# Third expert weight loaded from ScalarE's DMA queue instead of SyncE's

## What is computed

```python
def _expert_choice(h, router_w, w1, w3, w2):
    ...
    gate, idx = lax.top_k(aff.T, C)
    xe = xs[idx]
    he = jax.nn.silu(jnp.einsum('ecd,edf->ecf', xe, w1)) * jnp.einsum('ecd,edf->ecf', xe, w3)
    ye = jnp.einsum('ecf,efd->ecd', he, w2) * gate[..., None].astype(h.dtype)
    out = jnp.zeros_like(xs).at[idx.reshape(-1)].add(ye.reshape(-1, D))
    return out.reshape(B, L, D)
...
    x = x + gate2 * _expert_choice(h, lp['router_w'], lp['exp_w1'], lp['exp_w3'], lp['exp_w2'])
```

## Time and profile before

| | |
|---|---|
| median of 3 runs | 1870.99 us (1865.37 to 1871.74) |
| the profiled execution's own time | 1873.86 us |
| its span, first to last instruction | 1872.0 us |
| mean granted TensorE clock over the span | 0.967 |
| TensorE matmul busy | 1765.5 us (94%) |
| VectorE, ScalarE, GpSimd busy | 672.1, 350.8, 155.3 us |
| moved by DMA | 542.20 MB, of which 501.16 MB on SyncE's queue |

### The profile page before, as it was taken

The page is one execution under the profiler, slowest core; times in us unless marked ns, Lnnn a source line. Parts: engine busy times, 40 slices in busy tenths (PEclk is TensorE's granted clock), DMA queues, the critical chain, the costliest instruction groups (busy, mean ns, idle before and its releaser), DMA issues.

```text
span 1872.0 us, 50720 instructions
## 1 busy us (share of the span) xinstructions
PE 1765.5 (94%) x23010; PEld 1179.4 (63%) x23010; DVE 672.1 (36%) x1562; ACT 350.8 (19%) x781; POOL 155.3 (8%) x141
## 2 busy tenths in 40 slices
PE   5999988979999999999889998898999999999996
PEld 3776767846666666666557776686566666556653
DVE  5543767542121111112166367765121111112114
ACT  3410365310000000000142115722000000000001
POOL 0200030100000000000002002210000000000000
PEclk8999999979999999999979999998999999999996
DMA  9668201289999999999943722035999999999994
GB/s 357 216 219 314 92 2 46 102 320 415 395 401 399 405 397 405 398 401 399 362 131 137 269 71 91 5 121 200 399 398 397 400 396 406 395 402 398 395 372 158
DMA packets 91919, 542.20 MB, mean 290 GB/s; under 512 B 7536, under 2 KB 12658, under 8 KB 68676
## 3 DMA queue, kind: packets, MB, share of 16 engines
q1 hardware_dynamic: 80444, 501.16, 67.6%
q0 software_dynamic: 10464, 36.51, 6.8%
q10 hardware_dynamic: 808, 1.39, 0.2%
HBM read 515.50 MB, written 23.53 MB: 288 GB/s over the span
## 4 chain that ended last, share of the span: by engine, by line
PE 75%; DMA 14%; DVE 6%; ACT 2%; issue 2%; POOL 1%; ACTq 0%; DVEq 0%; SPq 0%; POOLq 0%
PE bank L1198 43%; DMA ring<-in_exp_w 12%; PE bank L848 11%; PE bank L1035 5%; PE bank L723 3%; PE bank L750 2%; PE bank L1056 1%; PE bank L994 1%; PE bank L1217 1%; PE bank L1073 1%; PE bank L979 1%; DMA arena_z<-xn_dram,icur 1%; PE bank L883 1%; PE bank L1106 1%; PE bank L789 1%
## 5 line engine op out<-in xcount | busy, mean ns | idle before, releaser
L1198 PE MATMUL bank<-ring,arena_u 128*32 128x256 f32 x12288 | 680.0, 381 | 1.9 <-DVE arena_u L2140 1.3
L1198 PEld LDWEIGHTS bank<-ring,arena_u 128*32 128x32 f32 x12288 | 399.5, 110 | 264.3 <-issue 6.0
L1198 PE MATMUL bank<-ring,arena_z 128*32 128x256 f32 x6144 | 340.6, 381 | 14.8 <-DMA ring<-in_exp_w 9.5
L1198 PEld LDWEIGHTS bank<-ring,arena_z 128*32 128x32 f32 x6144 | 205.5, 110 | 145.8 <-issue 11.1
L2172 DVE SCALAR_TENSOR_TENSOR arena_z<-bank,gateT,gate 80x512 f32<-80x512 f32 (+1 forms) x60 | 34.2, 609 | 560.1 <-PE bank L1198 560.1
L1512 ACT ACTIVATE arena_z<-bank 128x512 f32<-128x512 f32 x30 | 17.9, 597 | 623.5 <-PE bank L1198 623.5
L2149 DVE TENSOR_TENSOR arena_z<-arena_z,bank 128x512 f32<-128x512 f32 x64 | 48.5, 838 | 199.1 <-PE bank L1198 199.1
L1035 PE MATMUL bank<-ring_r 128*128 128x512 f32 x320 | 100.8, 396 | 0.3 <-DVE arena_h_r L1899 0.3
L677 POOL DMA_INDIRECT x_res<-arena_z,iscat x30 | 43.2, 1439 | 670.6 <-DVE arena_z L2175 670.6
L1523 ACT ACTIVATE arena_z<-bank 32x256 f32<-32x256 f32 (+1 forms) x90 | 34.0, 377 | 295.6 <-PE bank L1198 294.9
L848 PE MATMUL bank<-ring_r,arena_h_r 128*128 128x512 f32 (+1 forms) x240 | 87.2, 363 | 0.0
(11 more groups left out here) (303 smaller groups left out, 1906.4 us busy)
## 6 DMA issues: line engine op xcount, KB each, us to landing
ring<-in_exp_w SPq DMA_DIRECT2D x180, 2048.0 KB, 21.6
ring<-in_ada_w SPq DMA_DIRECT2D x23, 2048.0 KB, 9.5
ring<-in_exp_w SPq DMA_DIRECT2D x48, 512.0 KB, 14.3
ring<-in_w_in SPq DMA_DIRECT2D x7, 2048.0 KB, 19.4
ring<-in_w_out SPq DMA_DIRECT2D x2, 4096.0 KB, 13.0
x_res<-arena_z POOLq DMA_DIRECT2D x10, 512.0 KB, 3.3
xn_dram<-arena_u POOLq DMA_DIRECT2D x10, 512.0 KB, 2.9
arena_z<-x_res POOLq DMA_DIRECT2D x5, 512.0 KB, 3.8
```

What stands on the lines that cost most here:

```text
L1198: mm = pe.matmul(group_out(out, g, slice(q * 32, q * 32 + 32)), x(c, t), slot[s][:, c, w * QUARTER:(w + 1) * QUARTER], start=(c == 0 and g ...
```

## The change

ScalarE issues the loads of the third weight for experts 1 to 15; SyncE's loop loses them. The two waits and the two transfers for each load stay what they were. The load is placed in ScalarE's program ahead of `gated` of the same expert.

```diff
@@ SyncE
                 fill(0, "exp_w1", 1, 0)
-                fill(1, "exp_w3", 1, w3_at(0))
                 with sp.Fori(1, EXPERTS - 1) as e:
                     fill(0, "exp_w1", e + 1, w1_next_at(e) - 3)
                     fill(2, "exp_w2", e, w2_at(e) - 3)
-                    fill(1, "exp_w3", e + 1, w3_at(e))
                 fill(2, "exp_w2", EXPERTS - 1, w2_at(EXPERTS - 2))
@@ ScalarE
+                def w3_next(e):
+
+                    for h in range(2):
+                        act.wait_ge(chunk_used, AHEAD + chunks(l, w3_at(e), h * HALF + HALF - 1))
+                        act.dma_start(slot[1][:, h * HALF:(h + 1) * HALF, :],
+                                      i["exp_w3"][l, bass.ds(e + 1, 1)]
+                                      .rearrange("b (p c) n -> (b p) c n", p=P)[:, h * HALF:(h + 1) * HALF, :])\
+                            .then_inc(half_in[1][h], 16)
+
...
+                w3_next(0)
                 gated(w1_next_at(0), 1)
                 moved(0, 0)
                 with act.Fori(0, PAIRS - 1) as k:
                     for u in range(2):
                         e = k * 2 + 1 + u
+                        w3_next(e)
                         gated(w1_next_at(e), e + 1)
                         moved(e, 1 - u)
                 moved(EXPERTS - 1, 1)
```

## The result

The changed kernel takes 1896.1 us (median of 4 runs, 1886.4 to 1899.6) beside 1868.2 us for the kernel before: a ratio of 1.0137 on record, 95% interval 1.011 to 1.0164, some 26 us slower (the kernel before has a fourth run here, so its median is no longer the 1870.99 us of three). Measured again later on one chip with the other experiments it was 1.0141 (1.0124 to 1.0158). Lines have moved: L1196 is what was L1198, the expert matmuls; L1529 is ScalarE's new load.

A forecast was written before the change was run, and what follows sets the result against it. TensorE and DMA were both taken as close to the bound in the expert stages. Issue time 0, ScalarE 0, rate loss 0 and reordering 9.5 us per layer, 19 us in all, took 1871 to 1890 us; range 1870 to 1950.

The forecast's parts named there:

- reordering alone: Expert stages: third-weight loads go ahead of second-weight loads, 19 us slower in all, 1881 to 1895 us; chance 0.55.
- What bounds the stage: Expert stages: TensorE and DMA both close to the bound, DMA needing 1.4 to 1.9 us more per expert.
- Issue time at 0: SyncE loses 30 loads of two halves at 0.333 us each; gains nothing, since its queue waits for TensorE.
- ScalarE at 0: ScalarE's added waits and issues per expert, 0.33 to 0.66 us each, cost 0, covered by idle time before its Silu.
- no change: Rival for the expert loads: order of service doesn't matter, issue time saved is 0, so 1871 us; chance 0.16.
- The second weight's second half is overtaken: Expert stages: next third weight moves ahead of this earlier-issued half; 9.5 us per layer, ceiling 10.5, 19 us in all.
- One row of what I said would show: Changed profile: SyncE's first- and second-weight loads would take 26 us and more from earlier on.
- Mixing: Expert-stage loads on two queues: no rate loss taken; rival that mixing costs rate, +120 us, up to 2010 us; chance 0.25.
- the DMA engines never idle: Second way to the expert-stage sum: same work done by any time, up to 10.5 us of third weight going ahead per layer.
- The clock rival: Granted clock falling after TensorE stalls of 1.5 to 3 us: not counted, no size or chance given.

The follow-up runs named there:

- experiment 5: Kernel before and changed kernel, each with every expert's row transposes done four times: 1.0364 (1938.8 us) and 1.0379 (1942.9 us).
- Experiment 1: Kernel before, all loads on SyncE's queue, with the second weight's second half issued after the next third weight: 1.0111, 1890.4 us.
- light kernel: Kernel before with two thirds of the expert matmuls left out: 0.9844, 1839.2 us; the changed kernel cut likewise: 0.9927, 1855.5 us.
- experiment 6: Kernel before and changed kernel, each with two thirds of the expert matmuls left out: 0.9844 (1839.2 us) and 0.9927 (1855.5 us).
- experiment 2: Kernel before with ScalarE instead of SyncE issuing all three weights' loads from the second expert on, in the same order: 0.9998.
- experiment 8: The changed kernel measured once more against the kernel before, on the same chip as the one-queue reordering: 1.0141, 1892.5 us.
- 9: Kernel before with the second weight's second half issued late on one queue, run again beside the changed kernel: 1.0144, 1892.9 us.
- 3: Against the kernel before, only the third weight's first half is issued by ScalarE, its second half by SyncE: 1.0064, 12 us slower.
- 4: Against the kernel before, ScalarE issues the second weight's loads instead of the third's: 1.0085, 16 us slower.
- 7: Kernel before with two thirds of the expert matmuls left out and the second weight's second half issued late on one queue: 0.9898, 1847.8 us.
- padded kernel before: Kernel before with each expert's row transposes done four times: 1.0364, 1938.8 us.

## Why the prediction was right

Forecast were 1890 us and 1.0% slower; measured, 1896.1 us and 1.4%, just above the 1881 to 1895 that the prediction gave to reordering alone. Step by step:

*What bounds the stage.* Right. The stage has almost no room on either side, and experiment 5 shows that the room decides: with 2.7 us more of TensorE's work per expert (its chain has the transposes at 3.72 us instead of 1.05) the order of the loads no longer matters. I read from the growing landing times that DMA needs 1.4 to 1.9 us more per expert than TensorE. Experiment 1, where TensorE stalls in every expert, gives 33.96 us per expert over eleven experts, 1.7 us more than TensorE's 32.27. The light kernel of experiment 6 gives 33.1 us over ten, only 0.8 us more. The ends of the stalls in the chain of experiment 1, and those of the waits in the chain of the light kernel before:

```profile
509.37 7.98 PE bank L1199 x144
...
882.89 7.98 PE bank L1199 x144
```

```profile
524.79 2.81 PE bank L1200 x30
...
855.90 7.73 PE bank L1200 x60
```

So what each expert pays in the full kernel, once the stalls have set in, is as forecast, though loads alone, at 403 GB/s instead of 392, need less. Why the full kernel moves less was not settled.

*Issue time at 0, ScalarE at 0.* Right: its issues took 0.339 us, and experiment 2 puts three times as many on ScalarE without a loss. By the rule of the Trainium skill that the prediction drew on ("DMA: Bandwidth & Descriptors", "Issuing engines are not separate DMA queues") only issue time was at stake, and no change; the interleaving it speaks of is what cost some 26 us here, by reordering.

*The second weight's second half is overtaken.* Right in mechanism, and near in size. The term was 9.5 us per layer with a ceiling of 10.5. The waits ahead of the second weight grew from 3.8 and 5.7 to 12.3 and 13.1 us, so by 8.5 and 7.4 (by 8.7 and 9.8 in the trace of experiment 8). That all weight waits together grew by 20.6 us, close to the 19, is partly luck: 4.7 of them are the waits at the start of the stages, ahead of a first weight, and the prediction had no such term (in experiment 8's trace only layer 1 has such a wait, of 3.1 us). Stalls on the second weight were forecast from about 560 us, one or two per expert, and came from 605 us on, six in each layer. Experiments 1 and 9 make the price without a second queue, 3 about halves it, 4 moves it to another weight, 5 makes it vanish. One row of what I said would show was too broad: not all loads on SyncE's queue take 26 us and more, only the second half of the second weight does (29.7 us, its first half 22.6).

*Mixing.* I took no loss in rate, and the full kernel shows none beyond the order (8 against 9); the light kernel leaves 7 to 15 us open (6 against 7). The sum by "the DMA engines never idle" leaned on a DMA share of 1.01; that share stays there while the rate falls to 392 to 396, so it proves less than I took from it.

*The clock rival, not counted.* This is the missing term. The prediction ruled it out on one wait of 2.6 us, at the end of layer 0's stage, behind which the clock stayed at 1.00. The same wait ends layer 1's stage, and there the 192 records behind it took 1.7 us longer, in the very trace of before. The chain behind these two waits, before and then after:

```profile
922.01 10.61 PE bank L1198 x192
...
1830.86 12.30 PE bank L1198 x192
```

```profile
930.25 12.30 PE bank L1196 x192
...
1849.16 12.30 PE bank L1196 x192
```

After, both are slow, and so are three of the twelve stalls on the second weight (those that end at 674.61, 777.50 and 1695.54 us). That makes five against one, some 6.7 us, of which 5 us stand behind the new stalls; the other 1.7 us stand behind a wait that both kernels have, and may as well be chance. The busy time agrees: the second weight's matmuls were busy 175.0 us in layer 0 where they were 169.4 us before (both grouped by what they read), and 173.3 against 171.2 in layer 1, 7.7 us in all. Beside the 20.6 us of waits, less 1.6 us by which the other two products were less busy (339.4 and 339.1 against 340.4 and 339.7), that is 26 to 27 us. The stages themselves grew by 25.2 us: first to last expert matmul starts 539.9 and 540.1 us apart after, 525.6 and 529.2 before. What lies outside the stages took 12.6 us less in the trace after than in that of before (804.6 against 817.2 us); it varies that much over the traces of this case, though no edit touches it, and so two single totals can't show the price.

## What to carry to other kernels

A queue is an order. In this ring, but for the start of a stage, each load has the same time from slot free to data needed, and no other order that was tried beat one queue in the order of need. Moving one stream to another engine's queue let it overtake loads that were needed sooner, and cost nothing only where DMA had a lead. So before a load is moved, compare the landing times of the loads that it would overtake with the time until they are needed: here 17.5 to 27.4 us of 27.1, so there was little to give away.

## What was not expected of the hardware

The DMA share of a window does not tell whether the engines are full: with TensorE made slower (experiment 5) they moved 379 to 381 GB/s in the padded kernel before, and the share still read 0.98 and 0.99, against 1.01 at 403 GB/s.

```profile
430.00:870.00 440.00, 440.00 (x7597) 276.59 (x7592) 72.99 (x136) 24.91 (x62) 28.28 (x24) 0.99 0.98 379
1350.00:1790.00 440.00, 438.70 (x7533) 275.53 (x7536) 72.12 (x137) 26.20 (x63) 26.79 (x23) 0.98 0.99 381
```

And the granted clock can fall after a stall of 2.2 us in an otherwise busy stage (2.18 us ahead of 674.61), while after another of 2.9 us it did not (2.86 us ahead of 607.69); behind the same 2.6 us wait at the end of a stage it stayed at 1.00 in one layer and fell in the other.
